# Expert layers of a decoder step: the diagonals of gated activations on ScalarE instead of VectorE

## The reference

```
ids   = i1 * N_KEYS + i2
gates = softmax(c_top)
act = gelu(einsum('td,thkd->thk', xb, u_tab[ib])) * gb
out = einsum('thk,thkd->td', act, v_tab[ib])
```

## Time and profile before

| | us |
|---|---|
| median of 3 runs | 4011.06 (4002.5 to 4021.96) |
| the profiled execution, own time | 3983.27 |
| its span | 3981.4 |
| mean granted clock of TensorE in it | 0.923 |
| first gather of layer 0, of layer 1 | 454.39, 2529.68 |
| last dot of layer 0 begins, of layer 1 | 1877.51, 3956.62 |

### The profile page before, as it was taken

The page is one execution under the profiler, slowest core; times in us unless marked ns, Lnnn a source line. Parts: engine busy times, 40 slices in busy tenths (PEclk is TensorE's granted clock), DMA queues, the critical chain, the costliest instruction groups (busy, mean ns, idle before and its releaser), DMA issues. The chain is left out here.

```text
span 3981.4 us, 32064 instructions
## 1 busy us (share of the span) xinstructions
PE 3205.7 (81%) x11016; PEld 1634.5 (41%) x11016; DVE 2500.9 (63%) x6235; ACT 600.9 (15%) x1440; POOL 1269.5 (32%) x1099
## 2 busy tenths in 40 slices
PE   7967787888878887887798888688788778887886
PEld 6552333333333433332566566333333334333332
DVE  2872477776777776775223343567777777776775
ACT  1120111111111111110222132111111111111111
POOL 0000244444434444443000110244444443444443
PEclk9966899999999999999899899899999999999999
DMA  3010699999999999998300153899999999999998
GB/s 140 15 46 11 270 387 383 391 389 381 374 370 393 380 376 389 384 380 341 121 2 2 69 239 138 324 377 372 391 386 378 393 370 396 362 387 380 380 384 332
DMA packets 182751, 1192.63 MB, mean 300 GB/s; under 512 B 22992, under 2 KB 32896, under 8 KB 44982
## 3 DMA queue, kind: packets, MB, share of 16 engines
q0 software_dynamic: 154368, 1128.34, 71.5%
q1 hardware_dynamic: 25229, 60.56, 4.1%
q10 hardware_dynamic: 2992, 1.70, 0.2%
HBM read 1186.53 MB, written 4.46 MB: 299 GB/s over the span
## 5 line engine op out<-in xcount | busy, mean ns | idle before, releaser
L1281 PE MATMUL p_acc<-p_rows,p_diag 128*128 128x512 f32 (+1 forms) x4160 | 2047.4, 641 | 546.6 <-DVE p_diag L1099 534.2
L875 POOL DMA_INDIRECT p_rows<-in_peer_uv,p_ids x1024 | 1206.4, 1178 | 1639.7 <-PE p_acc L1281 1520.9
L1090 DVE CUSTOM_DVE_ANT_0 p_rows<-p_rows,p_x_n 128x1024 f32<-128x1024 f32 x1024 | 1238.3, 1222 | 458.8 <-DMA p_rows<-in_peer_uv,p_ids 457.2
L1281 PEld LDWEIGHTS p_acc<-p_rows,p_diag 128*128 128x128 f32 (+1 forms) x4160 | 801.7, 201 | 1671.0 <-issue 863.6
L1099 DVE TENSOR_SCALAR p_diag<-ident,p_acts,p_gates 128x128 f32<-128x128 f32 x1024 | 307.1, 342 | 226.5 <-ACT p_acts L947 226.5
L947 ACT ACTIVATE p_acts<-p_dots 128x2 f32<-128x2 f32 x520 | 99.9, 203 | 1219.7 <-DVE p_dots L1090 1219.5
L1230 PE MATMUL p_q_bank<-p_w_q,p_xT 128*128 128x256 f32 x1024 | 241.0, 390 | 19.4 <-issue 17.2
L1230 PEld LDWEIGHTS p_q_bank<-p_w_q,p_xT 128*128 128x128 f32 x1024 | 200.3, 196 | 74.8 <-issue 46.0
L923 ACT COPY p_q_rows<-p_q_bank 128x256 f32<-128x256 f32 x68 | 25.3, 372 | 723.4 <-PE p_q_bank L1230 715.5
L1791 POOL MEMSET d_one<- 1x1 f32 x1 | 0.1, 88 | 379.9 <-POOLq L60 379.9
L869 POOL MEMSET p_eps<- 128x1 f32 x2 | 0.2, 101 | 307.7 <-POOLq L60 307.7
(11 more groups left out here) (357 smaller groups left out, 2722.0 us busy)
## 6 DMA issues: line engine op xcount, KB each, us to landing
p_rows<-in_peer_uv,p_ids POOLq DMA_INDIRECT x1024, 8.8
p_w_q<-in_peer_w_q SPq DMA_DIRECT2D x16, 768.0 KB
a_arena<-in_ab_w_in SPq DMA_DIRECT2D x16, 512.0 KB, 9.0
a_arena<-in_ab_w_out SPq DMA_DIRECT2D x1, 4096.0 KB, 12.9
p_w_q<-in_peer_w_q SPq DMA_DIRECT2D x32, 128.0 KB, 3.4
c_w_out<-in_c_w_out SPq DMA_DIRECT2D x1, 4096.0 KB, 26.8
d_past<-in_c_w_out SPq DMA_DIRECT2D x1, 4096.0 KB, 14.2
c_w_in<-in_c_w_in SPq DMA_DIRECT2D x1, 2688.0 KB
```

Of the source, the lines that this page charges most:

```text
L875: nc.gpsimd.indirect_dma_start(out=rows[:, slot % RING, :], out_offset=None, in_=w[f"peer_uv{layer}"], in_offset=bass.IndirectOffsetOnAxis ...
L1090: last = nc.vector.tensor_tensor_reduce(rows[:, k % RING, 0:D_MODEL], rows[:, k % RING, 0:D_MODEL], x, 1.0, 0.0, ALU.mult, ALU.add, dots[: ...
L1281: last = nc.tensor.matmul(acc[done % 2][0:n, at], diag[:, slot // GROUP % 4, j, 0:n], rows[:, (slot + j) % RING, D_MODEL + 512 * b:D_MODEL ...
```

## The change

The two functions of DVE that make diagonals are taken out, and ACT does the work with a new function `weigh`. Behind the gelu of a group come four multiplications by a per-partition scalar: each of the two columns of `acts` times its gate into a new tile `gated`, then `ident` (or `own_row`, 8 columns) times each gated column into `diag`. The order of ACT is otherwise as before: where `gelu(i)` stood, gelu and the four multiplications stand. DVE makes dots and routing, and nothing waits on DVE between the dots of a group and its diagonals. Waits are added on ACT: for its own gelu and its own gated columns, for `rows_used` of the group four back (whose diagonals PE must have read), for the query's gates, and for the sample gates ahead of the sample slots.

```diff
+        gated = sb("gated", [128, 4, GROUP])
...
-            def gelu(i):
+            def weigh(slot, gate, unit=ident, n=128):
+
+                i = slot // GROUP
                 act.wait_ge(dotted, i + 1)
                 nc.scalar.activation(acts[:, i % 4, :], dots[:, i % 4, :], ACT.Gelu).then_inc(gelud, 1)
+                act.wait_ge(gelud, i + 1)
+                for j in range(GROUP):
+                    nc.scalar.mul(gated[:, i % 4, j:j + 1], acts[:, i % 4, j:j + 1], gate[:, j:j + 1]).then_inc(gated_ready, 1)
+                act.wait_ge(gated_ready, GROUP * (i + 1))
+                if i >= 4:
+                    act.wait_ge(rows_used, GROUP * (i - 3))
+                for j in range(GROUP):
+                    last = nc.scalar.mul(diag[:, i % 4, j, 0:n], unit[:], gated[:, i % 4, j:j + 1])
+                last.then_inc(diag_ready, 1)
+
+            def gelu(i):
+                n, k = divmod(GROUP * i - (H_P if GROUP * i >= SMP_SLOT else 0), TOPK)
+                weigh(GROUP * i, gates[:, n % (AHEAD + 1), k:k + GROUP])
...
                 if n == SMP_AT:
+                    act.wait_ge(smp_step, 6)
                     for g in range(H_P // GROUP):
-                        gelu(SMP_SLOT // GROUP + g)
+                        weigh(SMP_SLOT + GROUP * g, smp_gates[:, GROUP * g:GROUP * g + GROUP], own_row, DEC_BATCH)
...
+                act.wait_ge(gates_ready, route_no(n) + 1)
                 gelu(i)
                 gelu(i + 1)
...
-            def weigh(slot, gate):
-
-                i = slot // GROUP
-                dve.wait_ge(gelud, i + 1)
-                for j in range(GROUP):
-                    last = nc.vector.tensor_scalar(diag[:, i % 4, j, :], ident[:], acts[:, i % 4, j:j + 1], gate[:, j:j + 1], ALU.mult, ALU.mult)
-                last.then_inc(diag_ready, 1)
...
                     dot(slot, x)
-                    if g:
-                        weigh(slot - GROUP, gate[:, GROUP * g - GROUP:GROUP * g])
-                    elif n == SMP_AT:
-                        smp_weigh(slot - GROUP, smp_gates[:, H_P - GROUP:H_P])
-                    elif n:
-                        weigh(slot - GROUP, gates[:, (n - 1) % (AHEAD + 1), TOPK - GROUP:TOPK])
...
-            slot = first_slot(NW - 1) + TOPK - GROUP
-            weigh(slot, gates[:, (NW - 1) % (AHEAD + 1), TOPK - GROUP:TOPK])
             add_to_x(4, NT - 1)
```

More of the change, by code:

```diff
@@ L829, in peer_layer @@
         rows_in = [sem(f"rows_in{i}") for i in range(RING)]
-        dotted, gelud, diag_ready, rows_used, acc_used = (sem(n) for n in ("dotted", "gelud", "diag_ready", "rows_used", "acc_used"))
+        dotted, gelud, gated_ready, diag_ready, rows_used, acc_used = (sem(n) for n in ("dotted", "gelud", "gated_ready", "diag_ready", "rows_used", "acc_used"))
         R_STEPS = 18
@@ L1122, in sample_slots @@
                     dot(slot, x_smp[:])
[L1123 to L1127, removed]
                     if g == 2:
@@ L1147, in _ @@
                     dve.wait_ge(xn_ready, t + 1)
-                dve.wait_ge(gates_ready, route_no(n) + 1)
-                gate = gates[:, n % (AHEAD + 1), :]
                 for g in range(GROUPS):
```

## The result

The changed kernel takes 3788.92 us (median of 6 runs, 3783.22 to 3791.67) against 4004.05 (6 runs, 3993.99 to 4021.96): ratio 0.9457, interval 0.9435 to 0.9478. That is 215 us less; forecast were 3822 us and 188 less. The profiled execution took 3789.1 us, span 3787.3; forecast for it were 3795 and 3793.

The account below looks back on a forecast made before the run. Gathers into the ring were taken as the bound, delayed at query changes. Saving 64 x (4.06 - 1.2) = 183 us plus 5 in tails gave 188: 3795 us, scaled 3822; forecast 3744 to 3892, overall range 3740 to 3935.

Parts of the forecast that it names:

- rival B: Expert loops: transfers are bound anyway, as the 97% DMA share suggests; only the tails change, 4006 us; chance 0.05.
- the order, not DVE's relief: Expert loops: taking 312 us of multiplications off DVE matters little; diagonals following their own group's dots come 3.9 us earlier.
- The chain at the change of query: From T, the old query's last dot's end, to the new query's first free row: T + 13.0 instead of T + 16.3.
- D: Time from a group's last dot to PE's start, through ACT's gelu and multiplications: 1.7 us, ends 1.2 and 2.8.
- signs of being wrong: POOL's waits for PE as long with low windows (A), 382 GB/s with longer queue (B), D over 2.6 (C).
- the excess kept: Loop time above the gathers' floor remaining per query: 0 to 2.3 us, taken as 1.2, against 4.06 before.
- if its clock drops: Behind each projection: PE idles 2.1 us; a drop to its lower clock adds 1.5, making the gather 1.3 us late.
- The 1.0 us that the prediction could not resolve: Per query in the expert loops: the part of the 4.06 us excess beyond the 3.1 us late gather.
- Each tail: Each layer's end, from last dot to PE's end: 7.7 us becomes 5.4, 2.3 saved twice.
- The scaled point: Whole kernel: 3795 us for the profiled execution, scaled by the 0.7% of the runs' median above it: 3822 us.
- Rival C: Change of query: slower through ACT if D exceeds 2.6 us; two table loads a group give 4226 us scaled; chance 0.08.
- Rival A: The stall moves to PE, late releases stay late; about 3.2 us a query kept, 3950 us scaled; chance 0.07.

Follow-up runs that it names:

- the ring kernels: Ring length changed from eight places: the kernel before with nine, 3840.78 us; the changed kernel with seven, 3878.14 us, and with six, 4141.41 us.
- the two kernels that do one each: Against the kernel before: diagonals right behind their own dots but still on DVE, 3819.38 us; diagonals on ACT but one group late, 4180.59 us.
- The doses: Changed kernel plus a copy on ACT that nothing reads, between gelu and gated columns: 128x1024, 3888.24 us; 128x1920, 4072.96 us.
- the larger copy: Changed kernel plus an unread 128x1920 copy on ACT between gelu and gated columns: 4072.96 us, ratio 1.0181.
- the smaller: Changed kernel plus an unread 128x1024 copy on ACT between gelu and gated columns: 3888.24 us, ratio 0.9713.

## Why the prediction was right

**The bound.** The gathers set the pace and the queue was too short: shown by the ring kernels. The share of 97% was not saturation; rival B, for which it spoke, is out.

**The two steps.** That the order, not DVE's relief, would bring the gain is shown by the two kernels that do one each: 183 of 215 us, and none (that one is 178 us slower than before).

**The chain at the change of query.** First row free at T + 13.0 forecast, T + 12.75 found. D was 1.53 instead of 1.7, since pairs of instructions on ACT overlap (two of 0.394 in 0.69 us); the single durations were 0.394 and 0.287 against 0.367 and 0.294 from the earlier trace rows, and there are no new table loads. The prediction's signs of being wrong did not come: POOL's waits for PE fell from 1539.2 to 1328.0 us, and the median from issue to the waiting dot rose from 9.1 to 12.3 us, where 8.8 towards 12 was forecast from issue to landing. PE, the engine nearest to becoming the bound, was busy 670 of 800 us and not 721: the forecast had scaled 652.73 us that held matmuls at the lower clock (0.94 in that window, 0.99 now).

**The size.** The term that was mis-sized is the excess kept: 1.2 us a query forecast, (2633.3 - 2592.7) / 64 = 0.63 found. That is 36 us, the 219.3 saved in the loops against 183. The step in it that failed is "if its clock drops": behind an ordinary projection PE idled 1.80 us, not 2.1, and its next group took 3.70. It did drop at 6 of the 8 norms, where the idle time was 3.2. The 1.2 itself was the middle of a range and was read from no row. The 1.0 us that the prediction could not resolve stays so: the change it looked at is like the others (T + 16.3 is the median too). Each tail is 2.5 us shorter (3771.48 to the addition, less 3766.20, against 7.7), forecast 2.3.

That the unscaled 3795 comes within 6 us of the profiled 3789.1 is luck: the loops saved 36 us more than forecast, and the stretch between the layers, untouched, was 29 us longer than in the short profile of before. The scaled point, 3822, had that shortness put right by its 0.7%, and its 33 us of error are about the term above.

**The rule of the Trainium skill** against `mul` on ScalarE ("ScalarE: Activation LUTs", "Rules for kernel authors") holds as a statement on the engines: 0.394 + 0.287 us on ACT against 0.342 on DVE, each the mean of one. (The prediction's 0.300 is busy time by instruction, in which two that overlap count once; by that measure ACT has 0.587, (355.2 + 245.6) / 1024.) The prediction's estimates by that page, 0.28 and 0.39 us, came within 0.01 us of the 0.287 and 0.394 measured. The rule would have misled here, as DVE's time was not the bound; with the same order, moving the work to the slower engine was even worth 30 us. The likely cause is that DVE no longer stands and waits for the gelu (busy or waiting for it, it was taken for 767 of 800 us when it kept the work), but no run shows it by itself. In that kernel the first row is even free earlier, at T + 11.6 (median of the 56).

**Rival C** put the point where the change turns slower at D = 2.6. The doses show that there is one, between 2.5 and 3.2, and a straight line between them crosses 4004 us at about 2.95, an estimate. Its two extra table loads did not occur. **Rival A** did not occur in the changed kernel, but the kernel with the projection behind group 0 is a case of it: a stall moved to PE, 96 us.

## What to carry to other kernels

Where gathers into a ring set the pace, ask how long a row is held outside the queue, not which engine is busy: work placed one group earlier was worth about as much as one more buffer (183 and 162 us), and once the queue is full neither is worth anything more. Where two engines wait for each other in written-out order, put what the other needs next ahead of a wait for it. A busy share of DMA near 97% can hide a tenth of the rate; compare GB/s with the best stretch of the same loop.

## What the runs showed that I had not expected

TensorE's clock does not follow the idle time just before a group alone: after 3.21 us idle 8 matmuls took 6.60 us in the changed kernel (window clock 0.83), after 3.50 us idle they took 3.70 in the kernel with the larger copy. Of the 48 changes of query without a norm, 32 had the drop with the larger copy and 16 did not, all after the same 3.50 us of idle time; with the smaller it was 26 and 22, all after 2.75. What tells them apart I did not find.
